# The last layer norm of a decoder layer moved from feature tiles to transposed token tiles

## The chip, the cores and the metric

The kernel runs on one core of one Trainium2 chip. The metric is device time in microseconds (us), the median of several executions. The five engines have short names in what follows: PE (TensorE, with PEld for its weight loads), DVE (VectorE), ACT (ScalarE), POOL (GpSimd) and SP (SyncE, which here only issues DMAs).

## The reference, cut to what matters

One decoder layer works on 576 tokens (512 of a prompt, 64 of samples) of 1024 features each. Three branches are merged and projected to `h`, and the layer ends like this:

```python
ff_gate, ff_up = jnp.split(h @ lw['w_ffn_in'], 2, axis=-1)
y = layer_norm(ALPHA * h + (jax.nn.silu(ff_gate) * ff_up) @ lw['w_ffn_out'], lw['ln2_w'], lw['ln2_b'])
```

The layer norm takes mean and variance over the 1024 features of a token. `y` is returned with tokens as rows, in float32. The change concerns this last layer norm alone.

## The kernel before

**Layout.** Nearly everything lies with features in the 128 partitions and tokens along the free axis. `y` before its norm is the tile `pre_norm2` (in the code `Y[2]`): 8 feature tiles `c` of 128 features, each with 576 tokens, worked on in two halves of 288 tokens.

**The last outputs.** An output `("y", c, half)` is one feature tile of one half: 22 hidden tiles, three matrix products each (low part of the hidden by high part of the weights, high by low, high by high), so 66 products of 288 columns, added up in one PSUM bank. The outputs come in the order of `halves_order(5)`: both halves of tiles 0 to 4, then (5, 0), (6, 0), (7, 0), (7, 1), (6, 1), (5, 1). So the two outputs that PE works on last are (6, 1) and (5, 1), and each has three weight units of its own (8, 8 and 6 hidden tiles). A unit is loaded by SP, rounded by ACT to its high part `w_hi_out` (step `split_hi`), and DVE subtracts that from the raw values to get `w_lo_out` (step `split_lo`); both have to be there before PE starts on the unit. `split_hi` and `split_lo` of a unit are issued two units ahead of its use.

**After an output** DVE adds it to `ALPHA` times the saved `h`, which is kept as a high and a low part (L1830 and L1833, two operations that read `x_lo` and `x_hi`). This also frees the PSUM bank.

**The norm.** The sums over features cross partitions, so they go over PE. POOL adds feature tiles together (L1381), and PE multiplies that sum and the last tile by a matrix of 1/1024 (`mean`, L1177 and L1179). DVE subtracts the mean (`center`, L2226), ACT squares (L1739), PE adds the squares up (`var`: for half 0 after POOL has folded 8 tiles into one, L1393 and L1187; for half 1 over all 8 tiles, L1191), ACT takes logarithm and exponential for the reciprocal root (L1744, L1747), DVE scales (`norm`, L2235), ACT adds the bias (L1754). Then PE transposes to tokens (`store`, L1200), ACT and DVE copy one half of the features each out of PSUM (L1425, L2250), and SP stores (L1238), in six chunks of tokens with two buffers.

**What sets the order.** `schedule()` writes one list of steps; each engine's program walks through that list and issues its own part of each step. Each engine works strictly in its order, with waits on semaphores. Half 0 of the norm lies between the outputs (6, 1) and (5, 1); all of half 1 lies behind (5, 1):

```python
for c, half in halves_order(Y_TAIL):
    extras = {(KT - 2, 1): [("center", 2, 0), ("fold", 2)], (KT - 3, 1): [("var", 2, 0), ("norm", 2, 0)]}
    out(("y", c, half), extras=extras.get((c, half), ()))
    ...
summed()
steps += [("center", 2, 1), ("store", 0), ("var", 2, 1), ("store", 1), ("store", 2), ("norm", 2, 1)]
steps += [("store", i) for i in range(3, 6)]
```

## Time and profile before

| | us |
|---|---|
| median of 3 executions (lowest, highest) | 1128.26 (1127.31, 1130.38) |
| the profiled execution, its own time | 1126.59 |
| its span, first to last instruction | 1124.7 |
| PE busy in the span | 1062.6 (94%) |
| DVE, ACT, POOL busy | 729.2, 469.8, 210.9 |

The span is what the profile shows; 1.9 us of the execution's own time lie around it. The profiled execution was 1.7 us shorter than the median. Mean granted clock of PE: 0.981 of full speed. A row of the timeline gives start, length, engine, line and operation, with idle time before it and what ended that. Several equal instructions in a row are merged (x8), and their length then runs from the first start to the last end.

### The profile page before, as it was taken

The numbers are of one execution on the slowest core, as the hardware profiler recorded it, in microseconds if no ns is written. First come the engines' busy times: TensorE is split into PE (matmuls) and PEld (weight loads), VectorE is DVE, ScalarE is ACT, GpSimd is POOL, SyncE is SP. The second block draws the span as 40 slices with busy tenths as digits, with TensorE's granted clock in tenths as the row PEclk, the third lists the DMA queues.
The fourth block names the chain that finished last, engine by engine and source line by source line (L and its number), as shares of the span: only waits on it lengthen the run. The fifth ranks groups of instructions, "written<-read, shape, count | busy, mean of one in ns | idle before, by whom it ended". The sixth has DMA issues, their size and how long they took to land.

```text
span 1124.7 us, 19708 instructions
## 1 busy us (share of the span) xinstructions
PE 1062.6 (94%) x7888; PEld 1022.1 (91%) x7888; DVE 729.2 (65%) x1114; ACT 469.8 (42%) x896; POOL 210.9 (19%) x266
## 2 busy tenths in 40 slices
PE   6799999999999998899999998889999999999996
PEld 5799888987999997888999998789999999999985
DVE  4732376335668989874655578888888886632464
ACT  3533355542245453323422236555554544311245
POOL 3412000011146563463000033000000000010130
PEclk9899899999999999999999999999999999999998
DMA  9346111134321111133232346023233333222422
GB/s 272 81 136 224 42 53 57 57 100 142 117 75 47 49 58 56 57 109 108 76 94 76 102 142 169 1 60 110 83 106 88 101 94 90 71 85 72 135 85 84
DMA packets 166584, 105.82 MB, mean 94 GB/s; under 512 B 11976, under 2 KB 161152, under 8 KB 166480
## 3 DMA queue, kind: packets, MB, share of 16 engines
q1 hardware_dynamic: 160944, 85.01, 26.4%
q0 software_dynamic: 4896, 17.21, 4.8%
q10 hardware_dynamic: 656, 2.36, 0.6%
q8 instruction: 63, 1.03, 0.4%
q14 instruction: 25, 0.20, 0.1%
HBM read 98.60 MB, written 6.95 MB: 94 GB/s over the span
## 4 chain that ended last, share of the span: by engine, by line
PE 76%; DVE 12%; issue 4%; ACT 4%; POOL 2%; DMA 2%; SPq 0%; DVEq 0%; ACTq 0%; POOLq 0%
PE bank L816 12%; PE bank L817 12%; PE bank L818 12%; PE bank L891 6%; PE bank L894 6%; PE bank L893 6%; PE bank L848 3%; PE bank L846 3%; PE bank L847 3%; PE bank L1053 2%; DMA w_raw<-in_w_mem_kv 1%; DVE decay_q L2023 1%; PE bank L1036 1%; DVE w_lo L733 1%; DVE a_masked L2036 1%
## 5 line engine op out<-in xcount | busy, mean ns | idle before, releaser
L816 PE MATMUL bank<-x_lo,w_hi 128*128 128x288 f32 x864 | 265.5, 307 | 3.4 <-DVE x_lo L1933 2.7
L817 PE MATMUL bank<-x_hi,w_lo 128*128 128x288 f32 x864 | 255.0, 295 | 0.0
L818 PE MATMUL bank<-x_hi,w_hi 128*128 128x288 f32 x864 | 254.9, 295 | 0.0
L816 PEld LDWEIGHTS bank<-x_lo,w_hi 128*128 128x128 f32 x864 | 163.1, 189 | 11.8 <-issue 6.7
L817 PEld LDWEIGHTS bank<-x_hi,w_lo 128*128 128x128 f32 x864 | 163.1, 189 | 0.1
L818 PEld LDWEIGHTS bank<-x_hi,w_hi 128*128 128x128 f32 x864 | 162.6, 188 | 0.0
L733 DVE TENSOR_TENSOR w_lo<-w_raw,w_hi 128x1024 fp32r<-128x1024 f32 x66 | 83.3, 1266 | 66.7 <-ACT w_hi L1425 66.4
L1425 ACT ACTIVATE w_hi<-w_raw 128x1024 fp32r<-128x1024 f32 x88 | 92.3, 1054 | 57.6 <-PE bank L818 34.1
L891 PE MATMUL bank<-x_sum_lo,pair_hi 128*128 128x288 f32 x320 | 95.3, 298 | 6.3 <-DVE hidden L1822 2.6
L894 PE MATMUL bank<-x_sum_hi,pair_hi 128*128 128x288 f32 x320 | 94.8, 296 | 0.0
L1381 POOL TENSOR_TENSOR exp<-pre_norm 128x288 f32<-128x288 f32 x4 | 5.0, 1238 | 410.0 <-DVE pre_norm L1833 410.0
L733 DVE TENSOR_TENSOR w_lo_out<-w_raw_out,w_hi_out 128x1024 fp32r<-128x1024 f32 (+1 forms) x30 | 37.4, 1250 | 66.9 <-ACT w_hi_out L1425 66.9
L848 PE MATMUL bank<-hidden_hi,w_hi_out 128*128 128x288 f32 x264 | 77.8, 295 | 0.0
L846 PE MATMUL bank<-hidden_lo,w_hi_out 128*128 128x288 f32 x264 | 77.8, 295 | 0.0
L847 PE MATMUL bank<-hidden_hi,w_lo_out 128*128 128x288 f32 x264 | 77.7, 294 | 0.0
L733 POOL TENSOR_TENSOR w_lo<-w_raw,w_hi 128x1024 fp32r<-128x1024 f32 x22 | 58.2, 2648 | 87.6 <-ACT w_hi L1425 87.5
L891 PE MATMUL bank<-x_lo,pair_hi 128*128 128x288 f32 x240 | 70.5, 294 | 0.9 <-DVE weight_sums_lo L1903 0.9
L894 PE MATMUL bank<-x_hi,pair_hi 128*128 128x288 f32 x240 | 70.6, 294 | 0.0
L1425 ACT ACTIVATE w_hi_out<-w_raw_out 128x1024 fp32r<-128x1024 f32 (+1 forms) x30 | 29.6, 988 | 96.3 <-PE bank L848 80.6
L891 PEld LDWEIGHTS bank<-x_sum_lo,pair_hi 128*128 128x128 f32 x320 | 60.6, 189 | 7.3 <-issue 5.8
L894 PEld LDWEIGHTS bank<-x_sum_hi,pair_hi 128*128 128x128 f32 x320 | 60.7, 190 | 0.0
L816 PE MATMUL bank<-branch_lo,w_hi 128*128 128x288 f32 x192 | 59.3, 309 | 0.0
(307 smaller groups left out, 2720.3 us busy)
## 6 DMA issues: line engine op xcount, KB each, us to landing
w_raw<-in_w_in SPq DMA_DIRECT2D x46, 512.0 KB, 3.9
up_weights<-in_w_ffn_in SPq DMA_DIRECT2D x20, 512.0 KB, 3.9
gate_weights<-in_w_ffn_in SPq DMA_DIRECT2D x20, 512.0 KB, 5.0
w_raw_out<-in_w_ffn_out SPq DMA_DIRECT2D x20, 512.0 KB, 3.8
w_raw<-in_w_o SPq DMA_DIRECT2D x14, 512.0 KB, 3.8
w_raw<-in_w_mem_kv SPq DMA_DIRECT2D x8, 512.0 KB, 5.2
mem_ring<-in_mem_k_s POOLq DMA_DIRECT2D x8, 512.0 KB, 5.6
mem_ring<-in_mem_v_s POOLq DMA_DIRECT2D x8, 512.0 KB, 3.8
```

The source lines that it names most:

```text
L733: eng.tensor_tensor(lo_of_unit(u)[:, 0:n, :], raw_of(u)[:, 0:n, :], f32(hi_of_unit(u)[:, 0:n, :]), ALU.subtract).then_inc(w_lo_pool if u i ...
L816: pe.matmul(bank[:, 0:n], wh, lo, start=(i == 0), stop=False)
L817: pe.matmul(bank[:, 0:n], wl, hi, start=False, stop=False)
L818: mm = pe.matmul(bank[:, 0:n], wh, hi, start=False, stop=(i == len(parts) - 1))
L846: pe.matmul(bank[:, 0:TH], wh, lo, start=(i == 0), stop=False)
L847: pe.matmul(bank[:, 0:TH], wl, hi, start=False, stop=False)
L848: mm = pe.matmul(bank[:, 0:TH], wh, hi, start=False, stop=(i == len(parts) - 1))
L891: pe.matmul(bank[:, 0:TH], wh, xl[:, k, :], start=(first and k == 0), stop=False, skip_group_check=True)
L893: pe.matmul(bank[:, 0:TH], wl, xh[:, k, :], start=False, stop=False, skip_group_check=True)
L894: mm = pe.matmul(bank[:, 0:TH], wh, xh[:, k, :], start=False, stop=(k == KH - 1), skip_group_check=True)
L1053: mm = pe.matmul(bank[0:w, P * (i % 4):P * (i % 4) + w], k, q, start=True, stop=True)
L1425: return act.activation(dst, src, ACT.Copy)
```

## The change

The norm of `y` is done with tokens in the partitions, as the first layer norm of the kernel already is. PE transposes each block of 128 tokens (`TOKENS`: four of 128 and one of 64) by feature tiles into two PSUM banks of 512 features (`turn_y`). 37 of these 40 transposes stand inside the outputs (6, 1) and (5, 1), between two hidden tiles (`Y_TURNS`); only those of feature tile 5, for blocks 2, 3 and 4, come after the last output (`y_last`). DVE takes the statistics straight from PSUM (`y_stats`: `bn_stats` per bank, then `bn_aggr`), ACT the root, DVE the reciprocal. `y_norm` then scales: DVE does the first 512 features with two operations that read weight and bias as rows (`W2ROW`, `B2ROW`, loaded by two DMAs of POOL that copy one row into all partitions). Of the second 512 features ACT does the normalising and POOL multiplies by the weight row and adds the bias row; for block 3 alone DVE does both halves. SP stores each block in two halves. Before the output is there, DVE adds the two parts of `h` (now L1879), and after it there is a single operation (now L1882). Gone for this norm are the sums of POOL, the products with the matrix of 1/1024, centring, squaring, the logarithm and exponential, the scaling of feature tiles and the copies.

```diff
+Y_LATE = (2, 3, 4)
+Y_EARLY_C = [c for c in range(KT) if c != Y_TAIL]
+Y_TURNS = {(("y", KT - 2, 1), 8): (0, range(KT)), (("y", KT - 2, 1), 12): (1, range(KT)),
+           (("y", Y_TAIL, 1), 8): (2, Y_EARLY_C), (("y", Y_TAIL, 1), 12): (3, Y_EARLY_C),
+           (("y", Y_TAIL, 1), 16): (4, Y_EARLY_C)}
+Y_SHARED = (0, 1, 2, 4)
...
+    for key in [("y",) + x for x in halves_order(Y_TAIL)][:-2]:
+        out(key)
+    six, five = taken(("y", KT - 2, 1)), taken(("y", Y_TAIL, 1))
+    steps += six[:2] + [("y_stats", 0, 0), ("y_stats", 0, 1)] + six[2:4] + [("y_stats", 1, 0), ("y_stats", 1, 1)]
+    steps += [("y_norm", 0), six[-1]] + six[4:-1] + [("y_norm", 1)] + five[:-1]
+    steps += [("y_stats", t, 0) for t in Y_LATE] + five[-1:]
+    steps += [("y_last",)] + [("y_stats", t, 1) for t in Y_LATE] + [("y_norm", t) for t in Y_LATE]
...
+        y_banks = {0: (3, 4), 1: (5, 6), 2: (3, 4), 3: (5, 6), 4: (7, b7)}
...
+                    if (key, i) in Y_TURNS:
+                        turn_y(*Y_TURNS[key, i])
...
+            def turn_y(t, tiles):
+
+                t0, n = TOKENS[t]
+                for c in tiles:
+                    j = c // 4
+                    for half in range(2):
+                        if t0 < TH * half + TH and t0 + n > TH * half:
+                            pe.wait_ge(y_ready, Y_NO[2, half, c])
+                    bank = BANK[y_banks[t][j]] if y_parts[t][j] else take(y_banks[t][j], "yT", t, j)
+                    mm = pe.transpose(bank[0:n, P * (c % 4):P * (c % 4) + P], Y[2][:, c, t0:t0 + n], IDENT[:])
+                    y_parts[t][j] += 1
+                    if y_parts[t][j] == 4:
+                        mm.then_inc(y_turned[j], 1)
...
+                elif s == ("hidden_hi", LATE_HI[-1]):
+                    product_done(pool, "P4", PAIRS - 1)
+                    for row, name in ((W2ROW, "ln2_w"), (B2ROW, "ln2_b")):
+                        load(rows_in, row[:], a[name].unsqueeze(0).to_broadcast([P, D]))
+                elif s[0] == "y_norm" and s[1] in Y_SHARED:
...
+                    saved(pool, "yT", t, 1)
+                    pool.tensor_tensor(z, z, W2ROW[0:n, 512:D], ALU.mult).then_inc(z_scaled, 1)
+                    pool.wait_ge(z_scaled, i + 1)
+                    pool.tensor_tensor(z, z, B2ROW[0:n, 512:D], ALU.add).then_inc(z_shared, 1)
...
+                    act.wait_ge(y_shift, Y_SHARED.index(t) + 1)
...
+                    act.activation(OUTT[t % 4][0:n, 512:D], BANK[bank][0:n, :], ACT.Identity,
+                                   scale=BNR[0:n, t:t + 1], bias=ST[0:n, 0, t:t + 1]).then_inc(bank_free[bank], 1)
...
+                    dve.tensor_tensor(y, f32(XL[:, idx, cols]), f32(XH[:, idx, cols]), ALU.add).then_inc(x_whole, 1)
+                    dve.wait_ge(out_ready, OUT_NO[key] + 1)
+                    dve.wait_ge(x_whole, Y_NO[2, half, idx] - 2 * KT)
+                    dve.scalar_tensor_tensor(out=y, in0=y, scalar=ALPHA, in1=bank, op0=ALU.mult, op1=ALU.add)\
+                        .then_inc(bank_free[b], 1)
...
+                    dve.wait_ge(y_std, t + 1)
+                    step(dve.reciprocal(rstd, rstd))
+                    if t in Y_SHARED:
+                        dve.scalar_tensor_tensor(out=ST[0:n, 0, t:t + 1], in0=mean, scalar=-1.0, in1=rstd,
+                                                 op0=ALU.mult, op1=ALU.mult).then_inc(y_shift, 1)
...
+                    for j in range(1 if t in Y_SHARED else 2):
...
+                        dve.scalar_tensor_tensor(out=z, in0=BANK[bank][0:n, :], scalar=mean, in1=W2ROW[0:n, cols],
+                                                 op0=ALU.subtract, op1=ALU.mult).then_inc(bank_free[bank], 1)
+                        saved(dve, "yT", t, j)
+                        dve.scalar_tensor_tensor(out=z, in0=z, scalar=rstd, in1=B2ROW[0:n, cols],
+                                                 op0=ALU.mult, op1=ALU.add).then_inc((z_first, z_second)[j], 1)
```

**Where instructions moved.** PE in the output (5, 1), at the end of its first weight unit, before; the two kernels' line numbers differ, and `bank` without a number stands for any PSUM bank:

```order
L816 MATMUL bank<-hidden_lo_217,w_hi_out_185 128x288
L817 MATMUL bank<-hidden_hi_239,w_lo_out_184 128x288
L818 MATMUL bank<-hidden_hi_239,w_hi_out_185 128x288
L816 MATMUL bank<-hidden_lo_218,w_hi_out_186 128x288 [waits w_lo,w_hi]
L817 MATMUL bank<-hidden_hi_240,w_lo_out_181 128x288
L818 MATMUL bank<-hidden_hi_240,w_hi_out_186 128x288
```

and the same place in the changed kernel, where the seven transposes of token block 2 stand ahead of the second unit:

```order
L835 MATMUL bank<-hidden_lo_220,w_hi_out_188 128x288
L836 MATMUL bank<-hidden_hi_242,w_lo_out_187 128x288
L837 MATMUL bank<-hidden_hi_242,w_hi_out_188 128x288
L859 MATMUL bank<-ident,pre_norm_153 128x128 [waits bank_free3,y_ready]
L859 MATMUL bank<-ident,pre_norm_153 128x128 [waits y_ready] x3
L859 MATMUL bank<-ident,pre_norm_153 128x128 [waits bank_free4,y_ready]
L859 MATMUL bank<-ident,pre_norm_153 128x128 [waits y_ready] x2
L835 MATMUL bank<-hidden_lo_221,w_hi_out_189 128x288 [waits w_lo,w_hi]
L836 MATMUL bank<-hidden_hi_243,w_lo_out_184 128x288
```

The second unit now comes after transposes that wait for two PSUM banks and for the added-up tiles of half 1, (6, 1) among them.

DVE before, from the split of the first weight unit of output (5, 1) to the centring of half 1; L1830 and L1833 stand first for (6, 1), then for (5, 1):

```order
L733 TENSOR_TENSOR w_lo_out_184<-w_raw_out_180,w_hi_out_185 128x1024 [waits w_hi]
L733 TENSOR_TENSOR w_lo_out_181<-w_raw_out_177,w_hi_out_186 128x1024 [waits w_hi]
L1830 SCALAR_TENSOR_TENSOR pre_norm_153<-x_lo,bank 128x288 [waits out_ready]
L1833 SCALAR_TENSOR_TENSOR pre_norm_153<-x_hi,pre_norm_153 128x288 [waits bank_free2]
L733 TENSOR_TENSOR w_lo_out_182<-w_raw_out_178,w_hi_out_187 128x768 [waits w_hi]
L2235 SCALAR_TENSOR_TENSOR pre_norm_153<-pre_norm_153,vectors,gate_77 128x288 [waits bank_free7,ln_rstd]
L2235 SCALAR_TENSOR_TENSOR pre_norm_153<-pre_norm_153,vectors,gate_77 128x288 x7
L1830 SCALAR_TENSOR_TENSOR pre_norm_153<-x_lo,bank 128x288 [waits out_ready]
L1833 SCALAR_TENSOR_TENSOR pre_norm_153<-x_hi,pre_norm_153 128x288 [waits bank_free0]
L2226 TENSOR_TENSOR pre_norm_153<-pre_norm_153,bank 128x288 [waits mean_ready]
L2226 TENSOR_TENSOR pre_norm_153<-pre_norm_153,bank 128x288 x7
```

and in the changed kernel from the normalising of block 0 (`out_tokens_157`) over the sum for (6, 1) and the split of the second weight unit of (5, 1) to that of the third; `softmax_stats` is reused for the shift that ACT adds:

```order
L2320 SCALAR_TENSOR_TENSOR softmax_stats<-bn_mean_var,bn_rstd 128x1 [waits dve_step]
L2329 SCALAR_TENSOR_TENSOR out_tokens_157<-bank,bn_mean_var,ln_w_rows 128x512 [waits rows_in]
L2332 SCALAR_TENSOR_TENSOR out_tokens_157<-out_tokens_157,bn_rstd,ln_b_rows 128x512 [waits bank_free3]
L1879 TENSOR_TENSOR pre_norm_153<-x_lo,x_hi 128x288
L1882 SCALAR_TENSOR_TENSOR pre_norm_153<-pre_norm_153,bank 128x288 [waits x_whole,out_ready]
L1885 ISA [waits bank_free2]
L750 TENSOR_TENSOR w_lo_out_184<-w_raw_out_180,w_hi_out_189 128x1024 [waits w_hi]
L2318 RECIPROCAL bn_rstd<-bn_rstd 128x1 [waits y_std]
L2320 SCALAR_TENSOR_TENSOR softmax_stats<-bn_mean_var,bn_rstd 128x1 [waits dve_step]
L2329 SCALAR_TENSOR_TENSOR out_tokens_158<-bank,bn_mean_var,ln_w_rows 128x512
L2332 SCALAR_TENSOR_TENSOR out_tokens_158<-out_tokens_158,bn_rstd,ln_b_rows 128x512 [waits bank_free5]
L750 TENSOR_TENSOR w_lo_out_185<-w_raw_out_181,w_hi_out_190 128x768 [waits w_hi]
```

Both splits for (5, 1) used to stand together ahead of the sum for (6, 1); now the second and the third stand behind the normalising of a block of tokens each, and the sum for (6, 1) behind that of block 0.

ACT before, from the squares of half 0, behind the last unit of (6, 1):

```order
L1739 ACTIVATE squares_155<-pre_norm_153 128x288 [waits centered,product,var_ready]
L1739 ACTIVATE squares_155<-pre_norm_153 128x288 [waits centered] x6
L1739 ACTIVATE squares_155<-pre_norm_153 128x288 [waits bank_free7]
L1425 ACTIVATE w_hi_out_185<-w_raw_out_180 128x1024 [waits w_used,raw_in3]
L1425 ACTIVATE w_hi_out_186<-w_raw_out_177 128x1024 [waits w_used,raw_in0]
L1425 ACTIVATE w_hi_out_187<-w_raw_out_178 128x768 [waits out_ready,raw_in1]
L1744 ACT_TABLE_LOAD
L1744 ACTIVATE gate_77<-bank,eps 128x288 [waits var_ready]
L1747 ACT_TABLE_LOAD
L1747 ACTIVATE gate_77<-gate_77 128x288 [waits bank_free5]
```

and in the changed kernel, from that last unit on:

```order
L1472 ACTIVATE w_hi_out_190<-w_raw_out_182 128x768 [waits out_ready,raw_in2]
L1805 ACT_TABLE_LOAD
L1805 ACTIVATE bn_rstd<-bn_mean_var,eps 128x1 [waits y_var]
L1472 ACTIVATE w_hi_out_188<-w_raw_out_183 128x1024 [waits w_used,raw_in3]
L1805 ACTIVATE bn_rstd<-bn_mean_var,eps 128x1 [waits y_var]
L1814 ACTIVATE out_tokens_157<-bank,softmax_stats,bn_rstd 128x512 [waits y_shift]
L1472 ACTIVATE w_hi_out_189<-w_raw_out_180 128x1024 [waits w_used,raw_in0]
L1814 ACTIVATE out_tokens_158<-bank,softmax_stats,bn_rstd 128x512 [waits y_shift]
L1472 ACTIVATE w_hi_out_190<-w_raw_out_181 128x768 [waits out_ready,raw_in1]
```

The three units of (5, 1) followed each other directly; now a root or a normalising of 512 features stands ahead of each, and each of these waits for DVE.

## Rows read from the trace of the kernel before

**Rows 1.** Busy time by stretches: PE, PEld, DVE, ACT, POOL, then granted clock (PEclk).
```profile
1000.00:1078.50 78.50, 78.50 (x596) 78.50 (x595) 27.11 (x35) 15.91 (x16) 8.71 (x8) 1.00 0.34 101
1088.30:1091.00 2.70, 0.14 (x2) 0.01 (x1) 2.67 (x3) 1.58 (x2) 2.49 (x2) 1.00 0.15 46
1091.00:1094.60 3.60, 3.58 (x13) 3.31 (x14) 1.15 (x3) 2.77 (x4) 1.45 (x1) 0.53 0.02 5
1102.00:1111.00 9.00, 8.05 (x45) 5.98 (x43) 5.27 (x13) 6.49 (x12) 0.00 (x0) 1.00 0.14 58
```

**Rows 2.** Timeline of PE from 1078 us: start, length, then what.
```profile
1078.41 0.30 PE L848 MATMUL bank<-hidden_hi,w_hi_out 128*128 128x288 f32 x1
1078.54 0.65 PE L1177 MATMUL bank<-exp,ones 128*128 128x288 f32 x2
...
1088.16 0.29 PE L818 MATMUL bank<-hidden_hi,w_hi_out 128*128 128x288 f32 x1
1091.02 1.16 PE L1187 MATMUL bank<-squares,ones 128*128 128x288 f32 x2 [2.57 <-POOL squares L1393]
1092.22 0.44 PE L817 MATMUL bank<-hidden_hi,w_lo_out 128*128 128x288 f32 x1
1094.61 0.30 PE L818 MATMUL bank<-hidden_hi,w_hi_out 128*128 128x288 f32 x1
...
1101.78 0.29 PE L818 MATMUL bank<-hidden_hi,w_hi_out 128*128 128x288 f32 x1
1103.70 1.04 PE L1200 MATMUL bank<-ident,pre_norm 128*128 128x128 f32 x8
1109.00 1.91 PE L1200 MATMUL bank<-ident,pre_norm 128*128 128x128 f32 x16
```

**Rows 3.** Timeline of DVE: the last output, and the last copy.
```profile
1102.11 0.46 DVE L1830 SCALAR_TENSOR_TENSOR pre_norm<-x_lo,bank 128x288 f32<-128x288 f32 x1 [4.08 <-PE bank L818]
1120.49 0.68 DVE L2250 COPY out_tokens<-bank 64x512 f32<-64x512 f32 x1 [1.08 <-PE bank L1200]
```

**Rows 4.** Instructions of L1238, the stores of SP.
```profile
DMA to landing us min/median/max: 2.6/2.8/3.0
```

**Rows 5.** Groups of DVE by form: count, then busy us and mean ns of one.
```profile
L1903 DVE TENSOR_TENSOR up_weights_lo<-up_weights,pair_hi 128x1024 fp32r<-128x1024 f32 x20 | 24.4, 1221 | 0.8
L2107 DVE BATCH_NORM_STATS2 bn<-x_tokens 128x6 f32<-128x512 f32 x8 | 5.0, 671 | 0.0
L2250 DVE COPY out_tokens<-bank 128x512 f32<-128x512 f32 x3 | 2.1, 689 | 4.5 <-PE bank L1200 4.5
L2109 DVE BATCH_NORM_AGGREGATE bn_mean_var<-bn 128x2 f32<-128x12 f32 x4 | 0.8, 209 | 0.1
L2091 DVE RECIPROCAL lower_tmp<-lower_tmp 128x4 f32<-128x4 f32 x1 | 0.2, 178 | 0.0
```

**Rows 6.** Groups of ACT by form.
```profile
L1425 ACT ACTIVATE w_hi_out<-w_raw_out 128x1024 fp32r<-128x1024 f32 x20 | 21.2, 1059 | 69.4 <-PE bank L848 58.6 <-DMA w_raw_out<-in_w_ffn_out 10.8
L1425 ACT ACTIVATE out_tokens<-bank 128x512 f32<-128x512 f32 x3 | 1.8, 584 | 1.2 <-PE bank L1200 1.2
```

**Rows 7.** Timeline of POOL and of DVE in the first norm.
```profile
668.23 6.03 POOL L1393 TENSOR_TENSOR squares<-squares 128x1152 f32<-128x1152 f32 x3 [9.08 <-ACT squares L1739]
669.14 2.85 DVE L733 TENSOR_TENSOR w_lo<-w_raw,w_hi 128x1024 fp32r<-128x1024 f32 x1 [1.46 <-ACT w_hi L1425]
671.92 0.44 DVE L1830 SCALAR_TENSOR_TENSOR pre_norm<-x_lo,bank 128x288 f32<-128x288 f32 x1
672.39 1.20 DVE L1833 SCALAR_TENSOR_TENSOR pre_norm<-x_hi,pre_norm 128x288 f32<-128x288 f32 x1
```

**Rows 8.** Instructions of L1833, of L1381 and of L733 on POOL: ns min/median/max.
```profile
L1833 DVE SCALAR_TENSOR_TENSOR pre_norm<-x_hi,pre_norm x32: 457/458/1203, 636.3 to 1102.6; 128x288 f32<-128x288 f32 x32
...
L1381 POOL TENSOR_TENSOR exp<-exp,pre_norm x20: 802/832/1892, 645.6 to 1091.3; 128x288 f32<-128x288 f32 x20
...
L733 POOL TENSOR_TENSOR w_lo<-w_raw,w_hi x22: 2366/2434/3677, 24.9 to 529.1; 128x1024 fp32r<-128x1024 f32 x22
```

More of the change, by code:

```diff
@@ L385, in schedule, with taken @@
     steps += pair_steps()
-    for c, half in halves_order(Y_TAIL):
-        extras = {(KT - 2, 1): [("center", 2, 0), ("fold", 2)], (KT - 3, 1): [("var", 2, 0), ("norm", 2, 0)]}
-        out(("y", c, half), extras=extras.get((c, half), ()))
-        if not (c in Y_PAIRED and half):
-            summed()
-        pending.append(mean(2, Y_TAIL, half, c))
-        if (c, half) == (KT - 1, 1):
-            summed()
-    summed()
-    steps += [("center", 2, 1), ("store", 0), ("var", 2, 1), ("store", 1), ("store", 2), ("norm", 2, 1)]
-    steps += [("store", i) for i in range(3, 6)]
+    def taken(key):
+        n0 = len(steps)
+        out(key)
+        got = steps[n0:]
+        del steps[n0:]
+        return got
+    for key in [("y",) + x for x in halves_order(Y_TAIL)][:-2]:
+        out(key)
+    six, five = taken(("y", KT - 2, 1)), taken(("y", Y_TAIL, 1))
[3 more added lines that the diff above has]
+    steps += [("y_last",)] + [("y_stats", t, 1) for t in Y_LATE] + [("y_norm", t) for t in Y_LATE]
     return steps, number, beside
@@ L616, in build_decoder_layer @@
         ln_lo = [sem(f"ln_lo{i}") for i in range(2)]
-        out_dma = [sem(f"out_dma{i}") for i in range(2)]
+        out_dma = [sem(f"out_dma{i}") for i in range(4)]
         cache_moved, prompt_state_out = sem("cache_moved"), sem("prompt_state_out")
@@ L1190, in _ @@
                             pe.wait_ge(squared, 16 * (ln - 1) + 8 + c + 1)
-                            mm = pe.matmul(bank[:, 0:TH], ONES[:], SQR[ln][:, c, :], start=(c == 0), stop=(c == KT - 1))
+                            mm = pe.matmul(bank[:, 0:TH], ONES[:], SQR[:, c, :], start=(c == 0), stop=(c == KT - 1))
                     mm.then_inc(var_ready, 1)
-                elif what == "store":
-                    i = rest[0]
-                    t0, n = OUT_CHUNKS[i]
-                    for j in range(2):
-                        pe.wait_ge(ln_hi, 16 + 8 * (i // 3) + 4 * j + 4)
-                        bank = take((S0_, T1_)[i % 2] if j else (S1_, V_)[i % 2], "outT", i, j)
-                        for k in range(4):
-                            mm = pe.transpose(bank[0:n, P * k:P * k + P], Y[2][:, 4 * j + k, t0:t0 + n], IDENT[:])
-                    mm.then_inc(outT_ready, 1)
+                elif what == "y_last":
+                    for t in Y_LATE:
+                        turn_y(t, [Y_TAIL])
         @block.sync
@@ L1738, in _ @@
                             saved(act, "mean", ln, half)
-                        act.activation(SQR[ln][:, c, :], Y[ln][:, c, half * TH:half * TH + TH], ACT.Square)\
+                        act.activation(SQR[:, c, :], Y[ln][:, c, half * TH:half * TH + TH], ACT.Square)\
                             .then_inc(squared, 1)
```

100 lines of the change are left out of this document (65 added, 35 removed).

## The prediction

> **What bounds the kernel now.** I read the busy times by stretches first, then the timeline of PE where a stretch shows idle time, then that of DVE at the end.
>
> From 1000 to 1078.5 us PE is busy for 78.50 of 78.50 us at full clock [rows 1]. PE alone paces the outputs up to (7, 1): taking POOL's 8.71 us of sums out of there gives nothing, and DVE's new pair of operations per output (27.11 us busy) has room. Two later places are not paced by PE's work.
>
> The first lies between the last two outputs. The last product of (6, 1) starts at 1088.16, and PE's next instruction at 1091.02, after 2.57 us of waiting for POOL's fold of the squares [rows 2]. Then PE runs at a granted clock of 0.53 (the 1.2 GHz level) for 3.6 us [rows 1]: ten products take 1094.61 - 1092.22 = 2.39 us, 0.239 each, where the 54 that follow take 7.17 us, 0.133 each.
>
> The second is the tail. The last product starts at 1101.78 [rows 2], DVE takes that output up at 1102.11 [rows 3], and the span ends at 1124.7: 22.6 us in which the norm of half 1 passes between DVE, PE and ACT. The last copy ends at 1120.49 + 0.68 = 1121.17, so 3.5 us are the last store (2.6 to 3.0 until it has landed [rows 4]) and the end of the program. The profiled execution is 1102.1 + 22.6 + 1.9 outside the span = 1126.6. The median is 1.7 above it; I make the sum on the profile and add 1.7.
>
> **PE's stretch, if nothing waits.** It starts at 1078.54, where the products for the mean stand now [rows 2]. Two outputs are 132 products of 0.133: 17.5 us. A transpose costs (1.91 - 1.04) / 8 = 0.109 us [rows 2], so the 37 inside the outputs add 4.0. That ends at 1100.1, and DVE takes the last output up at about 1100.3 (0.33 after the start of the last product, as now), against 1102.1. Mean, variance, wait and slow clock were worth 5.8 us and the transposes take 4.0 of it back: a gain of 1.8.
>
> **What PE now waits for.** Each step of the norm stands ahead of work that PE needs. Block 0 is transposed by 1078.54 + 24 x 0.133 + 8 x 0.109 = 1082.6. DVE's second statistic (0.67) and the aggregate (0.21 [rows 5]) end near 1083.9. ACT's root (no row for one column; I take 0.25) and then its split of the first unit of (5, 1) (1.06 [rows 6]) end at 1085.2, DVE's part of it (1.22 [rows 5]) at 1086.5. PE wants that unit at 1089.0, so the root ahead of it costs nothing. DVE's two statistics and aggregate for block 1 end at 1088.1, reciprocal (0.18 [rows 5]) and shift at 1088.5.
>
> Here the engines fork. DVE's first scaling of 512 (no row; a copy of 512 from PSUM takes 0.69 [rows 5]) and ACT's normalising (a copy of 512 takes 0.58 [rows 6]) end together near 1089.2. Then DVE's second scaling and POOL's multiplication are ready within hundredths of each other, and both read two SBUF tiles. The first norm shows what happens then: beside POOL's fold, DVE's split of 1024 took 2.85 instead of 1.22, while L1830, with one operand in PSUM, kept its 0.44 [rows 5, 7]; L1833, with both in SBUF, took 1.20 instead of 0.46 [rows 7, 8]. POOL's sums stretched from 0.80 to 1.89 in turn [rows 8]. I read this as the two engines taking turns, one whole instruction each. A POOL operation of 512, alone, comes by the line through 288 (0.80) and 1024 (2.37) [rows 8] to 1.28.
>
> Turns with DVE first: DVE's scaling to 1089.9, POOL's multiplication to 1091.2, the sum L1879 for (6, 1) to 1091.6 and L1882 to 1092.1, POOL's addition to 1092.9, the split of the second unit of (5, 1) to 1094.1. PE comes to that unit at 1089.0 + 24 x 0.133 + 7 x 0.109 = 1093.0 and waits 1.1. The same round for block 1 then finds DVE's third split done before PE wants it. With POOL first, all is up to 1.3 later: the sum for (6, 1) is there at 1093.4 where PE wants it for its transposes at 1092.8, the second unit at 1094.7, and the third unit 0.6 late: 2.35 in all. So the last output is taken up between 1101.5 and 1102.65. The bounds are 1100.3, with no turns, and the wait of the second rival below. PE's gain is spent; what counts is the tail.
>
> **The tail**, counted from the last take-up. L1882 0.46, then a few hundredths to the no-op that reports it, PE's first transpose and its latency: DVE sees block 2 at about 1.1. Three rounds of statistic and aggregate (0.67 + 0.21 + waits 0.06): 3.9. Reciprocal and shift: 4.3. Two scalings for block 2: 5.7. Reciprocal and four scalings for block 3: 8.8. Reciprocal and shift of block 4: 9.2. From there the last chain is ACT (0.6) and POOL (2 x 1.28): 12.5. Turns between POOL's work on block 2 and DVE's scalings of blocks 2 and 3, and at block 4, add 1.7 (DVE first) to 2.3: 14.1 to 14.8. The last store is half as large as the last one now; I take 3.3 for it and the end (bounds: 2.6 landed and 0.5, and today's 3.5). The tail is 17.4 to 18.1 with turns, 15.8 without, against 22.6. Statistics of PSUM have no row; between 0.67 and the copy's 0.69 it makes no difference.
>
> **Costed at nothing.** The two row loads of POOL are issued before the 13 outputs ahead of (6, 1), that is 13 x 66 x 0.133 = 114 us before 1078.5, on a queue that has nothing else left. If they were late, DVE's first scaling would wait. The raw weights of the last units: their buffers come free as the transposes push the products back, so ACT finds them landed. The one table load of ACT stands in front of a root that waits 2 us for DVE.
>
> **Sum.** 1101.5 + 17.4 = 1118.9 to 1102.65 + 18.1 = 1120.75, middle 1119.8: 4.9 less than 1124.7. The profile would give 1121.7, the median 1128.26 - 4.9 = 1123.4.
>
> **Rivals.**
> No turns (POOL's operations fall between those of DVE): 1100.3 + 15.8 = 1116.1, time 1119.7. For it: ACT's end and DVE's first scaling are so close that small shifts decide. Against it: DVE has hardly a gap there.
>
> The clock drops after one long wait. Where the waits for the sum and the split of the second unit join, and POOL's operations take the 1.9 that they do at worst for 288 columns [rows 8], PE may stand still for 3 us; after 2.57 us of waiting the clock was at the slow level [rows 1, 2]. Price: 3 for the wait, and up to 24 remaining products plus transposes at 0.239 for 0.133, about 3: 1106.3 + 18.1 = 1124.4, time 1128: no change. Against it: the waits worked out are 1.1 to 1.7 in one piece.
>
> Slower: the transposes themselves cost PE its clock, from the first block on at 1081.7. Then 108 products cost 0.106 more each, 11.4, and the 37 transposes 4.0 more; DVE's waits vanish behind that: 1115.8 + 17.4 = 1133.2, time 1136.8. It decides from 10.4 us of such loss on, that is with two thirds of the stretch at the slow level. Against it: from 1102 to 1111, with 24 transposes in it, the clock was 1.00 [rows 1], and 16 in a row kept 0.109 [rows 2]. The Trainium skill (TensorE: Matmul & The Clock Gate, Part 4: PE-mode transpose) speaks for this rival: it states that the fast clock does not engage for transposes. By that rule the time would be this rival's 1136.8, by the rows the forecast's; the trace does not bear the rule out for short runs between products.
>
> **Chances.** Forecast 0.58 (its own range 1121 to 1125), no turns 0.18, clock drop 0.13, slow transposes 0.04, the rest, unnamed, 0.07. 0.3% is 3.4 us, about what this measurement can tell: the forecast and "no turns" lie below 1124.9. Faster 0.78, same 0.16, slower 0.06. A range from 1118.5 to 1127 takes in the forecast, no turns and half of the clock drop.
>
> **What would show it.** Right: PE without the 2.57 us wait, at clock 1.00 through (5, 1), transposes 0.11 apart; POOL's operations of 512 near 1.3 alone and up to 2 beside DVE; a PE wait of 1 to 2 us for the second or third split of (5, 1), released by DVE; the last output taken up near 1102; a tail of 17 to 18 us that ends with POOL. Wrong: PE waiting for PSUM banks, for the rows, or for ACT; a granted clock under 1.00 between 1082 and 1101; POOL's operations of 2 us or more alone; or stores that queue on SP.

## The result, and the profile after

The changed kernel takes 1117.95 us (median of 4 runs, 1116.64 to 1119.84), the kernel before beside it 1129.32 (1127.31 to 1132.20): ratio 0.9899, 95% interval 0.9871 to 0.9926. It is faster, by 11.4 us in these runs, and below the range of 1118.5 to 1127 that was given. Two later comparisons of the same kernels, with more runs, gave 0.9924 (0.9899 to 0.9948) and 0.9935 (0.9914 to 0.9957), with medians 7.8 and 8.7 us apart.

The profiled execution has a span of 1118.0 us against 1124.7. The two executions did not come to the changed place at the same time: the first product of (6, 1) starts at 1079.83, 1.29 later than what stood there before [rows 2]. So I count everything from there, and call the time from the start of (6, 1) to the end of the span the section. It was 1124.7 - 1078.54 = 46.16 us and is 1118.0 - 1079.83 = 38.17: **8.0 us less**, where 4.9 were forecast. The kernel before was profiled once, so its 46.16 is a single measurement; the medians of the two later comparisons differ by about as much.

Busy time by stretches, columns as in [rows 1]: the two outputs in two parts, then the tail.

```profile
1079.83:1089.83 10.00, 10.00 (x80) 10.00 (x79) 6.17 (x12) 3.98 (x6) 0.00 (x0) 1.00 0.40 118
1089.83:1102.09 12.26, 12.01 (x93) 11.56 (x91) 10.19 (x15) 2.85 (x4) 6.58 (x4) 1.00 0.30 108
1102.09:1118.00 15.91, 0.52 (x3) 0.28 (x3) 9.34 (x20) 2.36 (x5) 6.20 (x4) 0.60 0.24 82
```

PE is busy for 22.01 of 22.26 us at a granted clock of 1.00, where the kernel before had a wait of 2.57 and a stretch at 0.53 [rows 1, 2]. Its timeline has the transposes of block 0, between the products of (5, 1) those of block 2, and the three behind the last output:

```profile
1079.83 0.29 PE L835 MATMUL bank<-hidden_lo,w_hi_out 128*128 128x288 f32 x1
...
1083.03 1.03 PE L859 MATMUL bank<-ident,pre_norm 128*128 128x128 f32 x8
...
1093.56 0.93 PE L859 MATMUL bank<-ident,pre_norm 128*128 128x128 f32 x7
1094.69 0.37 PE L835 MATMUL bank<-hidden_lo,w_hi_out 128*128 128x288 f32 x1 [0.20 <-DVE w_lo_out L750]
...
1102.74 0.52 PE L859 MATMUL bank<-ident,pre_norm 128*128 128x128 f32 x3 [0.69 <-DVEq L1885]
```

One wait of PE is left ahead of the last output, 0.20 us for DVE's split. On DVE, the scaling of block 0, the sum and the eviction of (6, 1), that split, and then the tail:

```profile
1089.33 0.74 DVE L2329 SCALAR_TENSOR_TENSOR out_tokens<-bank,bn_mean_var,ln_w_rows 128x512 f32<-128x512 f32 x1
1090.11 0.75 DVE L2332 SCALAR_TENSOR_TENSOR out_tokens<-out_tokens,bn_rstd,ln_b_rows 128x512 f32<-128x512 f32 x1
1090.78 1.54 DVE L1879 TENSOR_TENSOR pre_norm<-x_lo,x_hi 128x288 f32<-128x288 f32 x1
1092.42 0.46 DVE L1882 SCALAR_TENSOR_TENSOR pre_norm<-pre_norm,bank 128x288 f32<-128x288 f32 x1
1092.92 1.62 DVE L750 TENSOR_TENSOR w_lo_out<-w_raw_out,w_hi_out 128x1024 fp32r<-128x1024 f32 x1
...
1099.97 0.43 DVE L1879 TENSOR_TENSOR pre_norm<-x_lo,x_hi 128x288 f32<-128x288 f32 x1
1102.09 0.45 DVE L1882 SCALAR_TENSOR_TENSOR pre_norm<-pre_norm,bank 128x288 f32<-128x288 f32 x1 [1.68 <-PE bank L837]
1103.08 0.70 DVE L2309 BATCH_NORM_STATS2 bn<-bank 128x6 f32<-128x512 f32 x1 [0.54 <-PE bank L859]
...
1105.54 0.10 DVE L2318 RECIPROCAL bn_rstd<-bn_rstd 128x1 f32<-128x1 f32 x1
...
1107.39 0.75 DVE L2329 SCALAR_TENSOR_TENSOR out_tokens<-bank,bn_mean_var,ln_w_rows 128x512 f32<-128x512 f32 x1
1108.18 0.78 DVE L2332 SCALAR_TENSOR_TENSOR out_tokens<-out_tokens,bn_rstd,ln_b_rows 128x512 f32<-128x512 f32 x1
...
1109.65 0.97 DVE L2332 SCALAR_TENSOR_TENSOR out_tokens<-out_tokens,bn_rstd,ln_b_rows 128x512 f32<-128x512 f32 x1
...
1111.58 0.74 DVE L2332 SCALAR_TENSOR_TENSOR out_tokens<-out_tokens,bn_rstd,ln_b_rows 64x512 f32<-64x512 f32 x1
```

POOL beside it, for blocks 0, 2 and 4:

```profile
1090.37 1.63 POOL L1439 TENSOR_TENSOR out_tokens<-out_tokens,ln_w_rows 128x512 f32<-128x512 f32 x1 [131.12 <-ACT out_tokens L1814]
1092.08 1.38 POOL L1441 TENSOR_TENSOR out_tokens<-out_tokens,ln_b_rows 128x512 f32<-128x512 f32 x1
...
1106.72 1.68 POOL L1439 TENSOR_TENSOR out_tokens<-out_tokens,ln_w_rows 128x512 f32<-128x512 f32 x1 [7.37 <-ACT out_tokens L1814]
1108.48 1.59 POOL L1441 TENSOR_TENSOR out_tokens<-out_tokens,ln_b_rows 128x512 f32<-128x512 f32 x1
1111.77 1.67 POOL L1439 TENSOR_TENSOR out_tokens<-out_tokens,ln_w_rows 64x512 f32<-64x512 f32 x1 [1.69 <-ACT out_tokens L1814]
1113.52 1.25 POOL L1441 TENSOR_TENSOR out_tokens<-out_tokens,ln_b_rows 64x512 f32<-64x512 f32 x1
```

The last store is SP's; the span ends 3.2 behind its start:

```profile
1114.80 0.50 SPq L1271 DMA_DIRECT2D out_y_s<-out_tokens  x1
```

The reader should see three things. DVE's sum at 1090.78 takes 1.54, where the same operation takes 0.43 with POOL idle (row at 1099.97): it ends 0.3 behind POOL's operation of 1090.37, which is over at 1092.00. That one took 1.63 for 1.25 (row at 1113.52) and had begun while DVE's of 1090.11 ran. I read this as the engines taking turns; experiment 6 shows them. L2329, which reads PSUM, never grows. And the last take-up, DVE's first operation on the last output, stands 22.26 us behind the start of (6, 1) (23.57 before [rows 2, 3]), the tail is 15.91 (22.6 before). Of the 8.0 us, 1.3 come from PE's stretch and 6.7 from the tail.

### The profile page after: what moved, and what is told of

Its sections match the earlier page's. It is cut to its first block, busy times and chain, and to the rows that moved or that the text cites. A ratio compares the mean times of both kernels' runs of the same rounds, so it can differ in the third digit from the quotient of the medians.

```text
span 1118.0 us, 19606 instructions
## 1 busy us (share of the span) xinstructions
PE 1049.8 (94%) x7854; PEld 1010.6 (90%) x7854; DVE 732.3 (65%) x1112; ACT 452.3 (40%) x860; POOL 200.7 (18%) x261
## 3 DMA queue, kind: packets, MB, share of 16 engines
q8 instruction: 63, 1.03, 0.4%
## 4 chain that ended last, share of the span: by engine, by line
PE 74%; DVE 15%; issue 3%; ACT 3%; DMA 1%; POOL 1%; SPq 1%; DVEq 0%; ACTq 0%; POOLq 0%
PE bank L835 12%; PE bank L836 11%; PE bank L837 11%; PE bank L926 6%; PE bank L928 6%; PE bank L929 6%; PE bank L883 3%; PE bank L881 3%; PE bank L882 3%; PE bank L1088 2%; DMA w_raw<-in_w_mem_kv 1%; PE bank L1071 1%; DVE decay_q L2085 1%; DVE a_masked L2098 1%; PE bank L1114 1%
## 5 line engine op out<-in xcount | busy, mean ns | idle before, releaser
L750 DVE TENSOR_TENSOR w_lo<-w_raw,w_hi 128x1024 fp32r<-128x1024 f32 x66 | 86.0, 1306 | 66.4 <-ACT w_hi L1472 66.1
L750 POOL TENSOR_TENSOR w_lo<-w_raw,w_hi 128x1024 fp32r<-128x1024 f32 x22 | 55.9, 2539 | 81.2 <-ACT w_hi L1472 81.2
L1354 POOL TENSOR_TENSOR decay<-hb 128x128 f32<-128x128 f32 (+1 forms) x124 | 51.7, 451 | 39.4 <-DVE decay_q L2085 32.8
```

The source lines that it names most:

```text
L750: eng.tensor_tensor(lo_of_unit(u)[:, 0:n, :], raw_of(u)[:, 0:n, :], f32(hi_of_unit(u)[:, 0:n, :]), ALU.subtract).then_inc(w_lo_pool if u i ...
L1354: pool.tensor_tensor(level_view(e[:, i, 0:w], m), v, v[:, :, m - 1:m].to_broadcast([P, w // (2 * m), 2 * m]), ALU.subtract)
```

## Experiments

The timed runs of one kernel lie 3 to 11 us apart, so effects of 1 us are read from the section of the profile, which repeats: 38.17, 38.19 and 38.24 in three executions of the changed kernel. In each trace with transposes between the products the start of (6, 1) is 3.2 us ahead of the first of them; otherwise it is read from its own row. The columns from "last take-up" to "section" are us behind that start. The ends of DVE and POOL are left out for the kernel before, and POOL's where it has no part in the scaling; two kernels have no ratio, because only the profiled execution was timed.

```
                          start    last     DVE     POOL   section   ratio to before
                         of (6,1) take-up   ends    ends             (95% interval)
before                   1078.54   23.57                    46.16
changed                  1079.83   22.26   32.49   34.94    38.17   0.9899 (0.9871, 0.9926)
changed again            1075.71   22.28   32.51   34.96    38.19   0.9924 (0.9899, 0.9948)
changed, third           1076.86   22.26   32.49   34.94    38.24   0.9935 (0.9914, 0.9957)
no sharing               1080.78   22.38   35.11            37.82   0.9931 (0.9907, 0.9954)
blocks 0 to 3 shared     1079.13   22.26   33.81   33.26    37.37   0.9912 (0.9889, 0.9936)
transposes all last      1082.21   17.75   36.82   39.27    42.59   0.9956 (0.9937, 0.9975)
transposed twice         1080.68   25.87   36.10   38.55    41.82   0.9966 (0.9955, 0.9977)
POOL busy beside         1080.10   22.38   36.12   37.25    40.50
order and shift          1078.25   22.32   32.67   33.79    37.05   0.9901 (0.9881, 0.9922)
POOL's waits early       1080.85   22.25   32.48   34.94    38.15
order, shift and waits   1077.92   22.33   32.68   33.80    37.08   0.9936 (0.9913, 0.9959)
blocks 0 to 2 shared     1081.72   22.25   33.86   30.24    36.58   0.9914 (0.9893, 0.9936)
```

**1. The changed kernel again**, twice, unchanged: is the gain in the section, or also ahead of it?

> The changed kernel once more, as it is. The section behind the start of (6,1) took 38.17 us in its first profile against 46.16 before, 8.0 less; the medians differ by 11.4. Theory A (the whole gain is made behind the start of (6,1), the rest is where executions happen to differ upstream): section 37.9 to 38.5 us again, start of (6,1) anywhere from 1077 to 1083, and the median 7 to 9 us below that of before in the long run, ratio about 0.993. Theory B (something ahead of (6,1) became faster too, for good): median again 11 to 12 below, ratio 0.990, and the start of (6,1), taken as each timed run's span less the section, 3 us earlier than in the runs of the kernel before.

> The changed kernel a third time, beside the last version on the same chip. Section 38.1 to 38.3 us, the median 7 to 11 us below that of the kernel before, ratio 0.990 to 0.994; the start of (6,1) where it happens to fall, 1075 to 1083.

Measured: sections 38.19 and 38.24, medians 1119.71 against 1127.55 and 1118.64 against 1127.32. That is theory A: 8 us, made behind the start of (6, 1); the ratio of the first comparison is the lowest of three. Theory B's own sign is absent: the median span less the section puts the start of (6, 1) at 1117.9 - 38.19 = 1079.7 in the changed kernel's runs of the first of these two and at 1125.5 - 46.16 = 1079.3 in those of the kernel before, where B wants it 3 us earlier. Where (6, 1) starts moves by 6.5 us over the thirteen executions of the table, from 1075.71 to 1082.21, and the execution before lies within. One thing that differs upstream is the granted clock (third number from the end). In the execution before:

```profile
340.00:348.00 8.00, 5.52 (x33) 5.32 (x32) 7.34 (x9) 3.19 (x8) 7.71 (x17) 0.79 0.24 68
...
500.00:506.00 6.00, 5.96 (x42) 4.70 (x39) 4.43 (x8) 0.27 (x1) 4.46 (x4) 1.00 0.45 108
```

and in the changed kernel's, whose program is the same there:

```profile
340.00:348.00 8.00, 5.53 (x45) 5.48 (x45) 7.70 (x11) 3.64 (x7) 6.39 (x15) 1.00 0.24 68
...
500.00:506.00 6.00, 6.00 (x19) 3.44 (x20) 4.89 (x4) 0.22 (x1) 5.33 (x3) 0.59 0.53 152
```

In the second and the third execution of the changed kernel, the same program throughout, the stretch from 500 to 506 ran at 1.00. The granted clock falls in other places from one execution to the next. How much of the 6.5 us it makes is not shown: up to the start of (6, 1) PE's busy time differs by 5.8 us among these executions (1024.1 to 1029.9), but its idle time by as much (49.2 to 54.7). A difference of two whole spans, one of each kernel, can so be some us off; the section of the changed kernel repeats to 0.07.

**2. No sharing.** VectorE scales both halves of all blocks.

```diff
-Y_SHARED = (0, 1, 2, 4)
+Y_SHARED = ()
```

> VectorE scales both halves of all five blocks; GpSimd and ScalarE take no part in the scaling. VectorE's tail gets 4 more operations of 0.75 us and loses 2 shifts of about 0.1; GpSimd's end, which now comes 2.45 us behind VectorE's, is gone. Theory A (turns between VectorE and GpSimd cost little, about 0.2 us in the tail): VectorE ends 2.6 us later, at about 12.9 us behind the last take-up instead of the 12.7 at which GpSimd ended: 0 to +0.8 us against the changed kernel, and the operations of two SBUF inputs take 0.74 to 0.76 each as they do beside GpSimd. Rival (GpSimd holds up VectorE for whole operations, as predicted): without it VectorE's rows lose 1.2 to 1.7 us in the tail, so this kernel is 0.5 to 1.5 us faster than the changed one. Ahead of the last take-up both let VectorE's splits (1.62 and 1.82 us beside GpSimd) go back to 1.23 and 0.96, and TensorE's wait of 0.2 us vanish.

Measured: section 37.82, 0.35 less than with sharing, between the two. VectorE ends 12.73 behind the last take-up, as theory A had it (12.9), and L2332 takes 0.74 to 0.75 throughout. TensorE's wait of 0.20 for the split is gone, but the last take-up is no earlier (22.38 for 22.26): the seven transposes of block 3 take 1.16, where they take 0.93 in the changed kernel. Three of them need the PSUM bank of block 1's second half, which VectorE's second L2329 for block 1 now frees, at 1097.70, half a us after the first of the seven has started. What neither theory had is the end: 2.67 us from the issue of the last store to the end of the span, where the changed kernel needs 3.2. Sharing the work with GpSimd and ScalarE in this form is worth nothing, by the section or by the medians (1120.41 and 1119.71).

**3. The transposes, all behind the last output.** The products of (6, 1) and (5, 1) run without a break; then forty transposes, all statistics, all scaling.

```diff
-Y_TURNS = {(("y", KT - 2, 1), 8): (0, range(KT)), ...
+Y_TURNS = {}
...
+    steps += six + five + [("y_last",)]
+    steps += [("y_stats", t, j) for t in (0, 1) for j in range(2)] + [("y_norm", 0), ("y_norm", 1)]
+    steps += [("y_stats", t, j) for t in Y_LATE for j in range(2)] + [("y_norm", t) for t in Y_LATE]
```

> All forty transposes, the statistics and the scaling of all blocks come behind the last output, none between its products. Theory A (a transpose between the products costs TensorE 0.109 us and nothing more, at the full clock): the last take-up comes 37 x 0.109 = 4.0 plus 0.4 of waits earlier, 17.8 us behind the start of (6,1); behind it 10 statistics (6.7), 12 scaling operations (9.0), 5 roots and shifts (1.8), 1.2 until the first transposed block, GpSimd's last 2.5 and the store's 3.2 make 24.4 instead of 15.9: about 4.1 us slower than the changed kernel, still 4 us faster than before. Rival (transposes between products cost the clock or their long start): the take-up comes 6 us or more earlier and the kernel is at most 2 us slower than the changed one.

Measured: the last take-up at 17.75 (17.8 by theory A), section 42.59, 4.4 more than the changed kernel and 3.6 less than before. The 37 transposes and the waits cost PE 22.26 - 17.75 = 4.5 us. So PE's stretch gained little because its transposes took back most of what the removed stall gave, as forecast, and having the transposes, blocks 0 and 1 of the norm and the first statistics of the others between PE's products is worth 4.4.

**4. Each of the 37 transposes twice.**

```diff
-                    mm = pe.transpose(bank[0:n, ...], Y[2][:, c, t0:t0 + n], IDENT[:])
+                    for _ in range(2 if len(tiles) > 1 else 1):
+                        mm = pe.transpose(bank[0:n, ...], Y[2][:, c, t0:t0 + n], IDENT[:])
```

> Each of the 37 transposes inside the last two outputs is issued twice into the same place; nothing else changes. Theory A (0.109 us each at the full clock, TensorE paces the stretch): the last take-up comes 37 x 0.109 = 4.0 us later less the 0.4 of waits that this covers, 25.9 to 26.3 us behind the start of (6,1), clock 1.00, tail 15.9: section 41.8 to 42.2 us against 38.17. Rival (transposes between products cost the fast clock once there are enough of them): a granted clock under 1.00 in the stretch and 8 us or more on the section.

Measured: last take-up 25.87, section 41.82, 3.65 more. The granted clock is 1.00 from 1078 to 1105. Theory A: the 37 more cost 0.10 each ((3.61 + 0.20)/37, the wait of 0.20 being covered), and 74 between the products cost no clock; the rival that the prediction gave 4 in 100 is out for this pattern.

**5. GpSimd beside a kernel without sharing.** Eight additions of 512 columns into spare memory, from block 2's root on.

```diff
+                elif s == ("y_norm", 2):
+                    pool.wait_ge(y_std, 3)
+                    for k in range(8):
+                        ...
+                        pool.tensor_tensor(spare, *rows, ALU.add).then_inc(z_scaled, 1)
```

> The kernel without sharing, with eight GpSimd additions of 512 columns of which nobody uses the result (two SBUF inputs, into spare memory), begun when block 2 has its root. Without them VectorE's operations in the tail take 0.74 to 0.75 us and the section is 37.82. Theory A (turns by whole operations, but only with VectorE operations of two SBUF inputs; one that reads PSUM runs beside GpSimd): L2329 stays at 0.75, L2332 takes 0.95 to 1.2 in most of its six places, the GpSimd operations 1.6 to 1.9; section 39 to 40.5. Rival 1 (turns with every operation): L2329 grows too, to 1.2 or more; section 42 or more. Rival 2 (the engines share the port piece by piece): both kinds grow by at most 0.1, section below 38.6.

Measured: L2329 (here L2337) stays at 0.73 to 0.75; L2332 (here L2340) takes 1.01, 0.97, 0.78, 0.97, 0.79 and 0.97. Two rows of DVE's timeline:

```profile
1107.79 0.74 DVE L2337 SCALAR_TENSOR_TENSOR out_tokens<-bank,bn_mean_var,ln_w_rows 128x512 f32<-128x512 f32 x1
1108.56 0.97 DVE L2340 SCALAR_TENSOR_TENSOR out_tokens<-out_tokens,bn_rstd,ln_b_rows 128x512 f32<-128x512 f32 x1
```

and GpSimd's:

```profile
1104.83 12.52 POOL L1449 TENSOR_TENSOR squares<-ln_w_rows,ln_b_rows 128x512 f32<-128x512 f32 x8 [145.30 <-ACT bn_rstd L1813]
```

VectorE loses 1.0 us over six such operations (36.12 against 35.11). GpSimd's eight additions take 1.25 to 1.71 each. I read this as GpSimd working while L2337 runs, so that only what is left over, 0.2 at four of the six places, is waited for. The section, 40.50, lies in theory A's range for another reason: GpSimd's last addition, whose result nobody uses, ends at 1104.83 + 12.52 = 1117.35, and the span ends 3.25 behind it.

**6. The turns by themselves**, behind the last store of the changed kernel: phase 2 reads one input from PSUM, phase 3 has one SBUF input, phases 0 and 1 have two.

```diff
+                    if phase == 2:
+                        ins = dve.scalar_tensor_tensor(out=z, in0=BANK[S0_][:]..., in1=rows[0], ...)
+                    elif phase == 3:
+                        ins = dve.tensor_scalar(z, rows[0], BNV[:, 0, 0:1], BNR[:, 0:1], ...)
+                    else:
+                        ins = dve.scalar_tensor_tensor(out=z, in0=rows[0], ..., in1=rows[1], ...)
```

> The changed kernel, with a measurement behind its last store, four stretches of eight VectorE operations of 512 columns: two SBUF inputs with GpSimd idle; the same beside four GpSimd additions of two SBUF inputs; PSUM and SBUF input beside four additions; one SBUF input (with two scalars of a column each) beside four additions. Its time is longer by the measurement and is not compared. Theory A (whole operations in turn where both engines read two SBUF tiles): alone 0.75 each, about 5.5 us for eight; beside GpSimd the eight and the four take the sum of both, 5.5 + 5.0 = 10.5 us less a few tenths, or four additions and four VectorE operations alternate in 7.5 us and the rest runs alone; PSUM input and single input: 0.75 or less each and GpSimd 1.25 to 1.28, as if alone. Rival 2 (piece by piece): 6 to 7 us for the second stretch, with all operations a little longer.

DVE's timeline: two SBUF inputs alone, beside GpSimd, then PSUM and SBUF, then one SBUF input, both beside GpSimd.

```profile
1116.27 5.39 DVE L2360 SCALAR_TENSOR_TENSOR pre_norm<-ln_w_rows,bn_rstd,ln_b_rows 128x512 f32<-128x512 f32 x8 [4.78 <-DMA out_y_s<-out_tokens]
1126.69 9.41 DVE L2360 SCALAR_TENSOR_TENSOR pre_norm<-ln_w_rows,bn_rstd,ln_b_rows 128x512 f32<-128x512 f32 x8 [5.04 <-POOL squares L1450]
1136.21 5.36 DVE L2355 SCALAR_TENSOR_TENSOR pre_norm<-bank,bn_mean_var,ln_w_rows 128x512 f32<-128x512 f32 x8
1141.67 7.55 DVE L2358 TENSOR_SCALAR pre_norm<-ln_w_rows,bn_mean_var,bn_rstd 128x512 f32<-128x512 f32 x8
```

and the four GpSimd additions beside the third and the fourth stretch:

```profile
1136.18 4.94 POOL L1450 TENSOR_TENSOR squares<-ln_w_rows,ln_b_rows 128x512 f32<-128x512 f32 x4 [2.61 <-DVE pre_norm L2360]
1141.65 5.47 POOL L1450 TENSOR_TENSOR squares<-ln_w_rows,ln_b_rows 128x512 f32<-128x512 f32 x4 [0.52 <-DVE pre_norm L2355]
```

and one operation of each engine out of the second stretch:

```profile
1127.36 1.75 DVE L2360 SCALAR_TENSOR_TENSOR pre_norm<-ln_w_rows,bn_rstd,ln_b_rows 128x512 f32<-128x512 f32 x1
1126.80 1.76 POOL L1450 TENSOR_TENSOR squares<-ln_w_rows,ln_b_rows 128x512 f32<-128x512 f32 x1
```

Two SBUF inputs: four additions cost VectorE 9.41 - 5.39 = 4.0 us, 1.0 each. A pair takes 1.67 from start to start (VectorE's begin at 1127.36, 1129.04, 1130.70 and 1132.37), where one of each alone makes 0.67 + 1.24 = 1.91: nearly whole operations in turn, cheaper than theory A's second form (7.5 for four pairs and 4 x 0.67 for the rest, 10.2), and GpSimd pays as well. With PSUM as one input, neither engine notices the other: 5.36, and 4.94, which is 1.24 each. The fourth stretch is a miss: an operation of one SBUF input takes 0.53 at the least, and up to 1.52 beside GpSimd, whose additions take 5.47/4 = 1.37 each. The Trainium skill (SBUF — State Buffer, Who interferes with whom) states all three: two SBUF inputs contend with GpSimd's reads, at most one does not outside the two-port modes, and `tensor_scalar` can enter those. The runs agree on who contends; whether the fourth stretch ran in such a mode, none shows.

**7. Block 3 shared instead of block 4**, with the stores in the order in which their halves should end (not shown here); then with a shift of one tensor input, and the shared half of block 3 stored ahead of the last half of block 4.

```diff
+Y_SHARED = (0, 1, 2, 3)
...
-    dve.scalar_tensor_tensor(out=ST[0:n, 0, t:t + 1], in0=mean, scalar=-1.0, in1=rstd, ...)
+    dve.tensor_scalar(ST[0:n, 0, t:t + 1], mean, rstd, -1.0, ALU.mult, ALU.mult)...
```

> Block 3 is shared instead of the last block, whose two halves VectorE scales alone, and the stores go out in the order in which their halves end. VectorE has the same number of operations in the tail, GpSimd's two last ones start about 3 us earlier and no longer end the kernel. By theory A (turns of about 0.2 us in the tail): VectorE ends at about 1112.5 on the changed kernel's scale, GpSimd at about 1113.2, the last store is issued at 1113.3 instead of 1114.8: 1.0 to 1.8 us faster than the changed kernel. By the rival (whole operations in turn) GpSimd's four operations now lie beside VectorE's last six and cost up to 1.25 us more: 0 to 0.5 us faster.

> The version with block 3 shared (section 37.37, where VectorE's shift of one column for block 3 took 1.03 us behind a GpSimd operation and the last store went out 0.55 us after the half it waited on), with the shift as an operation of one tensor input and two scalars, and the shared half of block 3 stored ahead of the second half of block 4. Theory A (turns only against two SBUF tensors): the shift takes 0.16, VectorE ends 0.3 to 0.9 earlier, the last store is issued 0.6 to 1.0 us earlier: section 36.4 to 36.9, median 1 to 2 us below the changed kernel's. Rival (GpSimd's four operations are the end either way): section 37.0 to 37.4.

Measured: 37.37, between both expectations. VectorE lost 0.87 us where it was not looked for, on the shift of a single column, which has two SBUF inputs, came while GpSimd worked and ended with GpSimd's operation:

```profile
1106.03 1.68 POOL L1442 TENSOR_TENSOR out_tokens<-out_tokens,ln_w_rows 128x512 f32<-128x512 f32 x1 [7.36 <-ACT out_tokens L1817]
1106.69 1.03 DVE L2323 SCALAR_TENSOR_TENSOR softmax_stats<-bn_mean_var,bn_rstd 128x1 f32<-128x1 f32 x1
```

With one tensor input, also beside GpSimd:

```profile
1105.26 1.68 POOL L1442 TENSOR_TENSOR out_tokens<-out_tokens,ln_w_rows 128x512 f32<-128x512 f32 x1 [7.37 <-ACT out_tokens L1817]
1105.92 0.21 DVE L2323 TENSOR_SCALAR softmax_stats<-bn_mean_var,bn_rstd 128x1 f32<-128x1 f32 x1
```

VectorE then ends 1.1 earlier (32.67 for 33.81). That is the shift's doing and not the stores': the second kernel of experiment 8 has the new shift with the first order of stores, and VectorE ends at 32.68 there. The section is 37.05, 0.3 less: the rival's range. GpSimd, 33.79, is now the end.

**8. GpSimd's end.** Five waits of its program, for stores long done, moved ahead of its scaling; alone, and with the shared block 3 and the new shift of 7 in the first order of stores.

> In every profile in which GpSimd has the last operations, the span ends 3.23 to 3.3 us behind the last of them, also where nobody uses its result; the last store, issued at the same time in the changed kernel, needs 2.67 us to the end where GpSimd is idle. Here GpSimd's five last waits (for stores of caches and states that are long done) stand ahead of its first multiplication instead of behind its last addition. Theory A (these waits are the greater part of the 3.25 us): the end is then set by the last store, section 37.5 to 37.8 against 38.17, and the span ends less than 3 us behind GpSimd's last operation. Rival (the 3.25 us are the end of GpSimd's program whatever stands there): section 38.1 to 38.2, 3.23 to 3.3 us again.

> The version with block 3 shared and the shift of one tensor input (section 37.05), with the second half of block 4 stored ahead of block 3's shared half, and GpSimd's five last waits moved ahead. VectorE's last operation ends 32.7 and GpSimd's 33.8 us behind the start of (6,1). Theory A (the waits are the greater part of GpSimd's end): the last store is issued at 33.9 and the section is 36.4 to 36.7. Rival (GpSimd's end is fixed at 3.25 us): 37.0 to 37.1, as it was. The median should be 1.1 to 1.8 us below the changed kernel's by A, 1.1 by the rival; both are within what the timed runs of these kernels scatter.

Measured: 38.15 and 37.08. Nothing changed, both rivals are right: wherever GpSimd has the last operation, the span ends 3.2 to 3.3 us behind it, also without these waits, and also where no store depends on it (experiment 5).

**9. Blocks 0 to 2 shared**, one line against the changed kernel.

```diff
-Y_SHARED = (0, 1, 2, 4)
+Y_SHARED = (0, 1, 2)
```

> The changed kernel with block 4 taken back from the sharing, and nothing else: VectorE scales both halves of blocks 3 and 4, GpSimd ends with block 2. Theory A (what ends the kernel is the later of GpSimd's last operation plus 3.25 us, whatever stands behind it, and VectorE's last operation plus about 2.75 us for the last store): VectorE has two operations of 0.75 more than in the changed kernel and one shift less, it ends at 33.7 to 34.0 us behind the start of (6,1), GpSimd at 30.5; section 36.4 to 36.8, the shortest of all versions, against 38.17 for the changed kernel and 37.05 for the one with block 3 shared. Rival (the 3.25 us belong to the last store, not to GpSimd): 36.9 to 37.3. In the median both are within the scatter of the runs, 1 to 2 us below the changed kernel.

Measured: 36.58, the shortest section, 1.6 less than the changed kernel's, as theory A had it. DVE's last row and SP's last:

```profile
1114.84 0.74 DVE L2332 SCALAR_TENSOR_TENSOR out_tokens<-out_tokens,bn_rstd,ln_b_rows 64x512 f32<-64x512 f32 x1
```

```profile
1115.61 0.50 SPq L1271 DMA_DIRECT2D out_y_s<-out_tokens  x1
```

From that issue to the end at 1118.3 it is 2.7. The median, 1118.53 against 1128.23, can't show 1.6 us; the kernel is faster than before, and against the changed kernel only by its section.

## Why the prediction was wrong

The direction, the place and the mechanism were right: DVE, with POOL, sets the tail, PE's part gains little, the clock stays at 1.00, the transposes cost 0.10 to 0.11 each (0.109), POOL's operation alone takes 1.25 (1.28 forecast), and POOL ends the kernel. What was off are two sizes, and both came out too dear.

**"Turns ... add 1.7 (DVE first) to 2.3" is the term that failed.** DVE did go first: ACT's normalising took 0.78 where 0.58 was taken. But in the tail the turns cost DVE 0.03 and 0.23 (rows at 1108.18 and 1109.65) and POOL's multiplication for block 4 0.42 (1.67 for 1.25): 0.7 in the chain that ends last. DVE's operations alternate between L2329, which reads PSUM, and L2332. The prediction had the reason in its own [rows 7], where L1830, with one operand in PSUM, kept its 0.44 beside POOL, but it gives no working for its 1.7. Experiments 5 and 6 show what it missed: a POOL operation costs DVE 1.0 where no PSUM operation lies between, and about 0.2 where DVE alternates.

**The sums of durations were too long.** Rows of DVE overlap the next by some hundredths: eight operations of 0.74 take 5.39, 0.67 each (experiment 6). From the last take-up, DVE saw block 2 at 0.99 (1.1 forecast), ended the statistics at 3.5 (3.9), and had block 4's shift at 8.8 (9.2). With the turns, POOL ends at 12.68, where 14.1 to 14.8 stood. The tail is 15.91 for 17.4 to 18.1. Of the 1.8 by which the middle, 17.75, is too long, 1.3 are the turns (0.7 for 2.0, the middle of 1.7 and 2.3) and 0.7 the durations (the shift without its turns comes at 8.5); ACT's slower normalising gives some 0.2 back.

**PE's waits "1.1", and "2.35 in all", were 0.20 at the split.** The same chain was early: by 0.3 us at the end of block 0's scaling, 0.5 at the sum for (6, 1) and 0.85 at the split of the second unit, which ended at 1094.54, on the forecast's scale 1093.25 instead of 1094.1. PE reached it later than worked out, at 1093.2 for 1093.0. Last take-up: 22.26 behind the start, 21.76 without any wait, 22.96 to 24.1 forecast.

Together: 1.3 for the middle of the take-up (23.5) and 1.8 for that of the tail (17.75) are the 3.1 by which the section's gain, 8.0, is above 4.9. That makes 1120.3; the other 2.3 us to 1117.95 are not in the section. The medians differ by 11.4, 7.8 and 8.7 in three comparisons, and executions scatter by 6.5 us ahead of (6, 1), so I put these 2.3 down to the scatter of four runs; no run shows it. Two sums of the prediction are a tenth off (1100.3 + 1.1 is 1101.4, 9.2 + 0.6 + 2.56 is 12.4), which changes nothing.

**The rivals.** "No turns" gave nearly the measured tail (15.8), but for a wrong reason: the turns are there. The clock drop did not come: PE's one wait ahead of the last output was 0.20, and the granted clock stayed at 1.00. The slow transposes are refuted by these rows and by experiment 4. **Costed at nothing:** rightly for the row loads, the raw weights and ACT's root (0.29). The store and end, 3.3, were 3.2, but they belonged to GpSimd and not to the store.
